# A hybrid attention and MLP block on one core: prefix and attention queues in another order, the weight splits of the attention on VectorE

## The chip, the cores and the metric

One NeuronCore of a Trainium2 chip runs the whole program. The metric is the device time of one execution in microseconds (us); for repeated runs the median is given. The engines are TensorE (PE), VectorE (DVE), ScalarE (ACT) and GpSimd (POOL), with SyncE (SP) for most DMA issues. Each works through its own queue in order, and they wait for each other by semaphores.

## What is computed

Two layers over one sequence of S = 512 tokens of width 1024, in fp32. Each layer computes (`x` the stream, cut from the reference):

```
xn = rms_norm(x, attn_norm)
nsa_q, kv_c, kv_s, kv_w, nsa_g, cq, ckv, k_rope_raw, gate_a, gate_b = split_cols(xn @ w_in)
o_a = nsa_attention(...)    # 8 heads, 2 KV groups: compressed, selected and window branch
o_b = mla_attention(...)    # 8 heads; q = rms_norm(cq) @ w_uq, kv = rms_norm(ckv) @ w_ukv, rope
merged = sigmoid(gate_a) * (o_a @ nsa_w_o) + sigmoid(gate_b) * (o_b @ mla_w_o)
x = x + merged @ w_out
x = x + square(relu(rms_norm(x, mlp_norm) @ w_up)) @ w_down
```

and a last `rms_norm` ends it. In the MLA branch every head's key has 64 columns of its own and 32 roped ones that all heads share (`k_pe`).

## The kernel before

**Splits.** PE multiplies in a rounded fp32 form (fp32r), and a product is made of three matmuls: high part by high part, high by rest, rest by high (L1447, L1448, L1449). So every operand is split once. A weight unit is 128x1024 fp32 (512 KB). SP loads it into one of two `stage` slots; ACT rounds it into `wsplit[:, 0]` (`split_hi`, L602); the rest, `stage` minus the rounded part, goes into `wsplit[:, 1]`. The rest is made by DVE (`split_lo`, L958) or by POOL (its `split_lo`, L495). Narrow units, for the compression weights, have slots of their own (`narrow`). All names ending in `_hi` are ACT's rounding copies, and those in `_lo` or `_rest` the subtractions on DVE or POOL.

**Prefix.** 29 items of the list `PREFIX` are projected one after another from the normed input: keys and values of the three branches (KC, VC, KS, V 0, KW, V 1), queries (Q 0 to 3), the MLA's inputs (CQ 0 to 2), MISC, five gates; the compression's units W1, W2K, W2V come between. At each item ACT and DVE run what the list's code puts there: evacuation, the next split, rotation of queries and keys (`swap`, L652, on ACT; `rotated`, L1031, L1035, L1043, on DVE), their splits (`q_hi`/`q_lo`, `k_hi`, `v_hi`/`v_lo`). POOL makes the key rests (L481). For the MLA's norm ACT squares the three CQ tiles into `csq` (L708); PE sums columns by matmuls against a vector of ones (`c_mean_squares`, L1589, fp32 matmuls of one column); ACT takes the root, DVE the reciprocal and diagonals (L1087, L1091), and PE spreads them (`c_spread`, L1597). `kc_hi` (ACT, L742) and `kc_lo` (DVE, L1132) split the compressed keys.

**Attention.** The loop has 106 steps for 96 jobs: 64 of the NSA branch, then 32 of MLA. A job passes through the steps by lags: scores S on PE and the row maximum on DVE (L1188) at its own step, exponentials on ACT (L771), the sum's reciprocal (DVE, L1193) and POOL's `scale` (L490) two steps later, both for two jobs at a time on even steps, the transposes T on PE (L1708) at 4, their split (ACT L766, DVE `probs_lo` L1198) at 5, the product with the values (L1732) at 7 and the output at 8. PE fills the gaps with the remaining projections: `FILL` gives four pieces of a unit to steps: gates first, `("MLA", 0)` behind GATE 11, more gates, then MLA 1, 2, WA 0, MLA 3, WA 1 to 3. An MLA unit projects queries (MQ), for `p < 2` also keys (MK) and values (MV) of head pairs; their evacuations run at the steps of `EMPTY_AT`: `mla_rotate` (DVE L1215), `mla_k` (L1237), `mla_v`.

`SPLIT_STEP` gives each of 20 units the step in which its slot is free: 0, 2, 6, 11, 16, 21, 27, 32, 37, 43, 48, 53, 65, 73, 79, 81, 87, 90, 96, 100. In the kernel before, POOL makes these rests at the top of the next step:

```
for u in SPLIT_STEP:
    if SPLIT_STEP[u] == i - 1:
        split_lo(u)
```

Behind it in a step POOL runs `scale` of two jobs, `output_rest` (L507), `mla_key_rest` (L516), loads and stores of gates, and `mla_query_rest` (L522). In `mla_begin(p)`, p < 2, ACT copies `k_pe` into the shared rows of `MK` (L792, twice) at the first step of MLA p, and POOL's `mla_key_rest(p)` makes their rests one step later. DVE's order in a step is: maximum, sums, `probs_lo`, small splits of the first steps (`vc_lo`, L1140, at 3), evacuations, `output_lo`, and in steps 3 to 8 `compressed_weights` (L1162 to L1177), which picks the selected blocks. PE's scores of job i wait for the maximum of job i - 2 and, for MLA jobs, for the query rest `MLO["MQ", ...]`.

**Behind the attention.** `mla_half`, the out tiles and the MLP in four quarters run with every split on DVE and little else there; POOL squares (L588).

Of the kernel before, what the change touches and what calls it, by code (L numbers as in the profile page):

```python
# [9 lines left out]
ALU = mybir.AluOpType  # L10
# [25 lines left out]
FIRST_GATE, EARLY = 5, 12  # L36
# [74 lines left out]

def tile_of(item, piece):

    name, i = item
    if name == "MLA":
        return [("MQ", i, 0), ("MQ", i, 1), ("MK", i, 0), ("MV", i, 0)][piece]
    if name == "WA":
        return ("A", 2 * i + piece // 2)
    return item
# [46 lines left out]
for i in range(STEPS):  # L166
    for t in EMPTY_AT[i] + EMPTY_AT[i - 1]:
        if (t[0] in ("MK", "MV")) == (t in EMPTY_AT[i]) and t[0] in ("MQ", "MK", "MV"):
            MHI[t] = len(MHI)
    for name, p in DURING + LATE:  # L170
        if name == "MLA" and p < 2:
            if FIRST_STEP[name, p] == i:
                MHI["PE", p] = len(MHI)
            if FIRST_STEP[name, p] == i - 1:
                MLO["PE", p] = len(MLO)
    for t in EMPTY_AT[i - 2]:
        if t[0] == "MQ":
            MLO[t] = len(MLO)
# [23 lines left out]
def build(nc, units, units_n, params, x_in, tables, cf32, cmasks, gates_dram, out):  # L202
    ctx = ExitStack()
    with ctx:
# [185 lines left out]
        s_csq, s_cms, s_crms, s_cdiag, s_cspread = sems("s_csq", "s_cms", "s_crms", "s_cdiag", "s_cspread")  # L390
        s_cf, s_chi, s_clo = sems("s_cf", "s_chi", "s_clo")
# [75 lines left out]
        def _(pool):  # L467
# [7 lines left out]
            for l in range(L):  # L475
# [34 lines left out]

                def mla_key_rest(p, scaled):
                    pool.wait_ge(s_scl, l * NJ + scaled)
                    u = max(v for v in SPLIT_STEP if SPLIT_STEP[v] <= FIRST_STEP["MLA", p])
                    split_done(pool, l, u)
                    pool.wait_ge(s_mhi, l * NMHI + (MHI["PE", p] + 1))
                    pool.tensor_tensor(MK[64:128, p % 2, :, 1, :], kpe[64:128, :].unsqueeze(1).broadcast_to([64, 2, S]),  # L516
                                       MK[64:128, p % 2, :, 0, :], ALU.subtract).then_inc(s_mlo, 1)
                    pool.wait_ge(s_mlo, l * NMLO + (MLO["PE", p] + 1))
# [29 lines left out]
                pool.wait_ge(s_kl, l * 2 + 2)  # L548
                for i in range(FIRST_GATE):
                    store_gate(i)  # L550

                for i in range(STEPS):
                    for u in SPLIT_STEP:
                        if SPLIT_STEP[u] == i - 1:
                            split_lo(u)
# [4 lines left out]
                    if 0 <= j < NJ - 1 and closes(j) is not None:  # L560
                        done = [u for u in SPLIT_STEP if SPLIT_STEP[u] < i]
                        if done:
                            split_done(pool, l, max(done))
                        output_rest(closes(j), min((i - LAG_SUM) // 2 * 2 + 2, NJ))
                    for p in range(2):
                        if FIRST_STEP["MLA", p] == i - 1:
                            mla_key_rest(p, (i - LAG_SUM) // 2 * 2 + 2)
# [31 lines left out]
        def _(act):  # L599
# [42 lines left out]
            for l in range(L):  # L642
# [145 lines left out]
                def mla_begin(p):  # L788
                    act.wait_ge(s_scores, l * NJ + QK_AFTER[p])
                    if p < 2:  # L790
                        for e in range(2):
                            ins = act.activation(MK[64:128, p, e, 0, :], kpe[64:128, :], ACT.Copy)  # L792
                        ins.then_inc(s_mhi, 1)
# [28 lines left out]
                for u, item in enumerate(PREFIX):  # L822
# [4 lines left out]
                    if 0 < u and u in BN and item != ("GATE", FIRST_GATE - 1) and (l, u) != (0, 1):  # L827
                        if name == "KW":
                            k_hi(0)
                        split_hi(l, BIG[BN[u] + 2])  # L830
# [5 lines left out]
                    if name == "KW":  # L836
                        copies(1)
                        swap(2)
                    if item == ("V", 1):
                        blocks_hi(1)  # L840
                        v_hi()
                        k_hi(1)
# [21 lines left out]
                    if item == ("GATE", 2):  # L864
                        kc_hi()
# [9 lines left out]
                for i in range(STEPS):  # L875
# [31 lines left out]
                    for p in range(PAIRS):  # L907
                        if FIRST_STEP["MLA", p] == i:
                            mla_begin(p)
                    if 10 <= i < 13:  # L910
                        c_hi(i - 10)
# [41 lines left out]
        def _(dve):  # L953
# [58 lines left out]
            for l in range(L):  # L1012
# [254 lines left out]
                for u, item in enumerate(PREFIX):  # L1267
# [40 lines left out]
                    if item == ("V", 1):  # L1308
                        blocks_lo(1)
                        v_lo()  # L1310
# [15 lines left out]
                    if item in ROPED and name != "KS":  # L1326
                        rotated(ROPED.index(item))
# [12 lines left out]
                for i in range(STEPS):  # L1340
                    if i < NJ:
                        max_of(i)
                    if i % 2 == 0 and 0 <= i - LAG_SUM < NJ:
                        sums_of(i - LAG_SUM)
                    if 0 <= i - LAG_SPLIT < NJ:
# [5 lines left out]
                    for t in EMPTY_AT[i]:  # L1351
# [6 lines left out]
                        if name == "MQ":  # L1358
                            mla_rotate(t[1], t[2])
# [7 lines left out]
                    if 0 <= j < NJ and closes(j) is not None:  # L1367
                        output_lo(closes(j))
                    if 3 <= i < 9:
# [75 lines left out]
        def _(pe):  # L1445
# [29 lines left out]
            for l in range(L):  # L1475
# [107 lines left out]
                def c_mean_squares():  # L1583
                    free(("CM", 0))
                    pe.wait_ge(s_csq, l * 3 + 3)
                    for kind, tiles in enumerate(((0, 1), (2,))):
# [105 lines left out]
                def scores(i):  # L1692
# [3 lines left out]
                    if i >= NSA_NJ and qt == QT - 1:  # L1696
                        pe.wait_ge(s_mlo, l * NMLO + (MLO["MQ", t, e] + 1))
# [300 lines left out]
```

## Time and profile before

| | before |
|---|---|
| median of 3 runs | 1541.52 us (1540.92 to 1542.46) |
| the profiled execution | 1544.23 us, of which the span is 1542.4 |
| PE busy in the span | 1510.6 us, 98% |
| DVE, ACT, POOL busy | 882.6, 717.9, 437.5 us |
| mean granted clock of TensorE | 0.996 of full speed |

The span goes from the first to the last instruction in the trace. Layer 0 has its prefix up to some 145 us, its attention to 365 and the rest to 775; layer 1 the same stages from there. "Idle before" is the time an engine stood before an instruction, and the arrow names what ended last among what it waited for. PE's matmuls overlap: one takes 0.39 us and the next begins 0.23 us after it.

### The profile page before, as it was taken

The page shows a single profiled execution, that of the slowest core. Times are in us where ns is not written, and L with a number is a line of the kernel's source. Part 1 is how long each engine was busy: PE and PEld are TensorE (multiplying, and loading weights), DVE is VectorE, ACT ScalarE, POOL GpSimd, SP SyncE. Part 2 cuts the span into 40 slices and gives each one's busy share as a digit, 9 for nine tenths or more (in the row PEclk, how much of TensorE's full clock was granted, in tenths as well). Part 3 has the DMA queues.
Part 4 walks back from the last instruction along what each step waited for, and adds up shares of the span by engine and source line. Part 5 has one row for each costly group of instructions (what it writes and reads, how often), then busy time and mean ns, then how long its engine had stood idle before and what let it go on. Part 6 is the DMA issues. An engine that isn't in the chain of part 4 may idle for free.

```text
span 1542.4 us, 21237 instructions
## 1 busy us (share of the span) xinstructions
PE 1510.6 (98%) x7412; PEld 1264.5 (82%) x7412; DVE 882.6 (57%) x1529; ACT 717.9 (47%) x1308; POOL 437.5 (28%) x455
## 2 busy tenths in 40 slices
PE   8999999999999999999999999999999999999998
PEld 6888888887888888888888788788878888888886
DVE  6864755766654444535557757566675535354453
ACT  6853777873432222222366547777644212222222
POOL 1301666775020100101021036768730201010011
PEclk9999999999999999999999999999999999999999
DMA  5333212125333323323323422122343333323233
GB/s 208 105 128 123 90 62 76 45 91 173 96 96 96 96 95 95 98 94 97 107 83 123 151 81 83 55 69 58 98 148 94 96 96 96 97 94 105 92 101 110
DMA packets 43363, 154.31 MB, mean 100 GB/s; under 512 B 5440, under 2 KB 5440, under 8 KB 43280
## 3 DMA queue, kind: packets, MB, share of 16 engines
q1 hardware_dynamic: 37296, 133.77, 27.9%
q0 software_dynamic: 5696, 18.94, 3.5%
q8 instruction: 48, 0.79, 0.2%
q10 hardware_dynamic: 288, 0.52, 0.1%
q14 instruction: 35, 0.29, 0.1%
HBM read 142.73 MB, written 10.49 MB: 99 GB/s over the span
## 4 chain that ended last, share of the span: by engine, by line
PE 85%; DVE 5%; ACT 4%; issue 4%; DMA 1%; POOL 1%; SPq 0%; POOLq 0%; DVEq 0%; ACTq 0%
PE G L1447 14%; PE G L1449 13%; PE G L1448 13%; PE O L1449 9%; PE O L1448 9%; PE O L1447 9%; PE O L1732 3%; PE T L1708 3%; PE S L1683 2%; PE T L1447 2%; PE T L1449 2%; PE T L1448 2%; PE O L1522 1%; ACT wsplit L602 1%; DVE F L1388 1%
## 5 line engine op out<-in xcount | busy, mean ns | idle before, releaser
L602 ACT ACTIVATE wsplit<-stage 128x1024 fp32r<-128x1024 f32 x227 | 240.2, 1058 | 606.7 <-PE G L1449 281.2
L958 DVE TENSOR_TENSOR wsplit<-stage,wsplit 128x1024 fp32r<-128x1024 f32 x178 | 256.8, 1443 | 72.9 <-ACT wsplit L602 72.7
L588 POOL TENSOR_TENSOR F<-Y 128x512 f32<-128x512 f32 x64 | 68.4, 1069 | 637.4 <-DVE Y L1405 637.4
L1447 PE MATMUL G<-xg,wsplit 128*128 128x512 f32 x592 | 237.9, 402 | 10.0 <-DVE wsplit L984 6.8
L1448 PE MATMUL G<-xg,wsplit 128*128 128x512 f32 x592 | 232.1, 392 | 0.0
L1449 PE MATMUL G<-xg,wsplit 128*128 128x512 f32 x592 | 231.9, 392 | 0.0
L495 POOL TENSOR_TENSOR wsplit<-stage,wsplit 128x1024 fp32r<-128x1024 f32 x48 | 115.8, 2412 | 128.1 <-ACT wsplit L602 126.9
L1188 DVE CUSTOM_DVE_ANT_0 F<-S,F 128x512 f32<-128x512 f32 x192 | 93.6, 488 | 98.7 <-PE S L1683 62.0
L1447 PEld LDWEIGHTS G<-xg,wsplit 128*128 128x128 f32 x592 | 112.0, 189 | 32.8 <-DVE wsplit L984 6.8
L771 ACT ACTIVATE F<-F,nmx 128x512 f32<-128x512 f32 x192 | 107.7, 561 | 64.3 <-DVE nmx L1188 62.9
L1449 PEld LDWEIGHTS G<-xg,wsplit 128*128 128x128 f32 x592 | 111.7, 189 | 24.5
L1448 PEld LDWEIGHTS G<-xg,wsplit 128*128 128x128 f32 x592 | 112.0, 189 | 20.9 <-issue 0.7
L1447 PE MATMUL G<-area,wsplit 128*128 128x512 f32 x320 | 124.7, 390 | 0.3
L1449 PE MATMUL G<-area,wsplit 128*128 128x512 f32 x320 | 124.5, 389 | 0.0
L1447 PE MATMUL O<-area,wsplit 128*128 128x512 f32 x320 | 124.5, 389 | 0.0
L1448 PE MATMUL O<-area,wsplit 128*128 128x512 f32 x320 | 124.5, 389 | 0.0
L1448 PE MATMUL G<-area,wsplit 128*128 128x512 f32 x320 | 124.5, 389 | 0.0
L1449 PE MATMUL O<-area,wsplit 128*128 128x512 f32 x320 | 124.5, 389 | 0.0
L1198 DVE TENSOR_TENSOR area_b<-T,area_b 128x512 fp32r<-128x512 f32 x192 | 92.8, 484 | 26.2 <-ACT area_b L766 23.9
L1447 PE MATMUL O<-xg,wsplit 128*128 128x512 f32 x256 | 99.6, 389 | 0.0
L1448 PE MATMUL O<-xg,wsplit 128*128 128x512 f32 x256 | 99.6, 389 | 0.0
L1449 PE MATMUL O<-xg,wsplit 128*128 128x512 f32 x256 | 99.6, 389 | 0.0
(291 smaller groups left out, 3005.3 us busy)
## 6 DMA issues: line engine op xcount, KB each, us to landing
stage<-units SPq DMA_DIRECT2D x229, 512.0 KB, 3.5
stage_n<-units_n SPq DMA_DIRECT2D x20, 512.0 KB, 3.6
gates<-Y POOLq DMA_DIRECT2D x32, 256.0 KB, 2.6
E<-gates POOLq DMA_DIRECT2D x24, 256.0 KB, 3.7
F<-gates POOLq DMA_DIRECT2D x8, 256.0 KB, 4.0
x<-x_in SPq DMA_DIRECT2D x3, 512.0 KB, 6.4
rope<-tables POOLq DMA_DIRECT2D x1, 768.0 KB, 6.9
out<-F SPq DMA_DIRECT2D x3, 256.0 KB, 2.3
```

The lines of the kernel that those rows point to most:

```text
L495: pool.tensor_tensor(wslot(u)[:, 1, :], staged(u), wslot(u)[:, 0, :], ALU.subtract)\
L588: pool.tensor_tensor(F[:, m % 2, :], Y[:, m % 2, :], Y[:, m % 2, :], ALU.mult)\
L602: act.activation(wslot(u)[:, 0, :], staged(u), ACT.Copy).then_inc(s_whin if u in SN else s_whi, 1)
L771: act.activation(prob(i, w), prob(i, w), ACT.Exp, bias=nmx[:, i % 4:i % 4 + 1], scale=-1.0, accum_out=sums[:, i % 4:i % 4 + 1]).then_inc(s ...
L958: dve.tensor_tensor(wslot(u)[:, 1, :], staged(u), wslot(u)[:, 0, :], ALU.subtract)\
L1188: dve.tensor_tensor_reduce(prob(i, w), score_tile(i), maskrow[:, S - w:S], -1.0, 1e38, ALU.add, ALU.min, nmx[:, i % 4:i % 4 + 1]).then_inc ...
L1198: dve.tensor_tensor(pt_view(slot, 1, qt), tp_view(j % 2, qt), pt_view(slot, 0, qt), ALU.subtract)\
L1447: pe.matmul(dst, a(0), b(0), start=first, stop=False)
L1448: pe.matmul(dst, a(0), b(1), start=False, stop=False)
L1449: return pe.matmul(dst, a(1), b(0), start=False, stop=last)
L1708: ins = pe.transpose(TP[j % 2][:, kt * P:(kt + 1) * P], prob(j, S)[:, kt * P:(kt + 1) * P], ident)
L1732: ins = pe.matmul(dst[:, kt * P:S], v, PT[:, slot, c, kt * S:(kt + 1) * S - kt * P], start=opens and c == 0, stop=closes(j) is not None an ...
```

## The change

1. **Splits of the attention.** POOL's loop no longer makes the 20 rests. DVE makes each at the end of the same step, after `output_lo` and before `compressed_weights`. POOL keeps its split for V 0 in the prefix and three behind the attention. Its waits on splits go; a wait `rests_done` for its own older query rests takes their place.
2. **MLA 0.** `EARLY` goes from 12 to 13: GATE 12 is projected in steps 32 to 36, and MLA 0 in 37 to 41 (before: MLA 0 in 32 to 36, GATE 12 behind it). Its evacuations move with it.
3. **Shared key rows.** ACT's two copies leave `mla_begin` and run at `KEY_STEP` = 43 and 69, and POOL's rests at 44 and 70; before, they ran at 32 and 65, and at 33 and 66. The scores of the MLA jobs now wait for the rest of their key pair by name too.
4. **DVE's order in a step.** `mla_rotate` comes ahead of `probs_lo`.
5. **Prefix.** ACT's `swap(2)` and DVE's `rotated(2)`, KW's rotation, move from KW's item to V 1's; `k_hi(1)` moves from V 1's item to Q 0's; `kc_hi` moves ahead of the split in GATE 2's item.
6. **The mean square of CQ.** POOL adds `csq[1]` to `csq[0]` once (128x512), behind its last key rest of the prefix, and PE sums the columns of two tiles instead of three: 8 fp32 matmuls instead of 12.

The tables and their steps:

```diff
-FIRST_GATE, EARLY = 5, 12
+FIRST_GATE, EARLY = 5, 13
...
+KEY_STEP = [FIRST_STEP["MLA", 0] + 6, FIRST_STEP["MLA", 1] + 4]
```

On POOL:

```diff
+                def rests_done(i):
+                    rests = [MLO[t] for t in MLO if t[0] == "MQ" and EMPTY[t] + 2 < i]
+                    if rests:
+                        pool.wait_ge(s_mlo, l * NMLO + (max(rests) + 1))
...
+                pool.wait_ge(s_csq, l * 3 + 2)
+                pool.tensor_tensor(csq[:, 0, :], csq[:, 0, :], csq[:, 1, :], ALU.add).then_inc(s_csum, 1)
                 for i in range(FIRST_GATE):
                     store_gate(i)
 
                 for i in range(STEPS):
-                    for u in SPLIT_STEP:
-                        if SPLIT_STEP[u] == i - 1:
-                            split_lo(u)
...
                     for p in range(2):
-                        if FIRST_STEP["MLA", p] == i - 1:
+                        if KEY_STEP[p] == i - 1:
+                            rests_done(i)
                             mla_key_rest(p, (i - LAG_SUM) // 2 * 2 + 2)
```

On ACT:

```diff
                     if 0 < u and u in BN and item != ("GATE", FIRST_GATE - 1) and (l, u) != (0, 1):
                         if name == "KW":
                             k_hi(0)
+                        if item == ("GATE", 2):
+                            kc_hi()
                         split_hi(l, BIG[BN[u] + 2])
...
                     if name == "KW":
                         copies(1)
+                    if item == ("V", 1):
                         swap(2)
-                    if item == ("V", 1):
                         blocks_hi(1)
                         v_hi()
+                    if item == ("Q", 0):
                         k_hi(1)
...
+                        if p < 2 and KEY_STEP[p] == i:
+                            mla_key_hi(p)
```

On DVE:

```diff
                     if item == ("V", 1):
+                        rotated(2)
                         blocks_lo(1)
                         v_lo()
...
+                    for t in EMPTY_AT[i]:
+                        if t[0] == "MQ":
+                            mla_rotate(t[1], t[2])
                     if 0 <= i - LAG_SPLIT < NJ:
                         probs_lo(i - LAG_SPLIT)
...
                         output_lo(closes(j))
+                    for u in SPLIT_STEP:
+                        if SPLIT_STEP[u] == i - 1:
+                            split_lo(l, u)
                     if 3 <= i < 9:
                         compressed_weights((i - 3) // 3, (i - 3) % 3)
```

On PE:

```diff
+                    pe.wait_ge(s_csum, l + 1)
-                    for kind, tiles in enumerate(((0, 1), (2,))):
+                    for kind, tiles in enumerate(((0,), (2,))):
...
                     if i >= NSA_NJ and qt == QT - 1:
-                        pe.wait_ge(s_mlo, l * NMLO + (MLO["MQ", t, e] + 1))
+                        pe.wait_ge(s_mlo, l * NMLO + (max(MLO["MQ", t, e], MLO["PE", min(t, 1)]) + 1))
```

The lines of the changed kernel stand a little lower: DVE's L958 is its L966, L1140 its L1148, L1162 its L1170, L1188 its L1196, L1198 its L1206; POOL's L490 is its L493, L507 its L510, L516 its L522, and L522 its L528.

The order of DVE's instructions in layer 0's steps 3 and 4, before (`vblk` is `vc_lo`'s result, ISA with `nmx` the row maximum):

```order
L1140 TENSOR_TENSOR vblk<-O,vblk 32x2x64 x4
L1162 TENSOR_TENSOR E<-E,constf 128x512
L1188 ISA F,nmx<-S,F 128x512
L1188 ISA nmx 128x1
L1193 RECIPROCAL rsum<-sums 128x2
L1165 TENSOR_REDUCE small<-E 128x16
L1167 TENSOR_SCALAR small<-small 128x16
L1169 RECIPROCAL small<-small 128x16
L1188 ISA F,nmx<-S,F 128x384
L1188 ISA nmx 128x1
L1198 TENSOR_TENSOR area_b<-T,area_b 128x4x128
```

and now:

```order
L1148 TENSOR_TENSOR vblk<-O,vblk 32x2x64 x4
L966 TENSOR_TENSOR wsplit<-stage,wsplit 128x1024
L1170 TENSOR_TENSOR E<-E,constf 128x512
L1196 ISA F,nmx<-S,F 128x512
L1196 ISA nmx 128x1
L1201 RECIPROCAL rsum<-sums 128x2
L1173 TENSOR_REDUCE small<-E 128x16
L1175 TENSOR_SCALAR small<-small 128x16
L1177 RECIPROCAL small<-small 128x16
L1196 ISA F,nmx<-S,F 128x384
L1196 ISA nmx 128x1
L1206 TENSOR_TENSOR area_b<-T,area_b 128x4x128
```

One row is new there, the weight unit's rest between `vc_lo` and `compressed_weights`; the row maxima and `probs_lo` come one instruction later.

POOL's order around the second key rest, before (`F<-F,rsum` rows are `scale`, `area<-kpe,area` the key rest, `area<-E,area` the query rests, `wsplit` a weight unit's rest):

```order
L495 TENSOR_TENSOR wsplit<-stage,wsplit 128x1024
L490 TENSOR_SCALAR F<-F,rsum 128x512
L490 TENSOR_SCALAR F<-F,rsum 128x384
L516 TENSOR_TENSOR area<-kpe,area 64x2x512
L490 TENSOR_SCALAR F<-F,rsum 128x256
L490 TENSOR_SCALAR F<-F,rsum 128x128
L522 TENSOR_TENSOR area<-E,area 128x512 x2
L490 TENSOR_SCALAR F<-F,rsum 128x512
L490 TENSOR_SCALAR F<-F,rsum 128x384
L490 TENSOR_SCALAR F<-F,rsum 128x256
```

and now, from the same `scale` rows before the query rests on:

```order
L493 TENSOR_SCALAR F<-F,rsum 128x256
L493 TENSOR_SCALAR F<-F,rsum 128x128
L528 TENSOR_TENSOR area<-E,area 128x512 x2
L493 TENSOR_SCALAR F<-F,rsum 128x512
L493 TENSOR_SCALAR F<-F,rsum 128x384
L522 TENSOR_TENSOR area<-kpe,area 64x2x512
L493 TENSOR_SCALAR F<-F,rsum 128x256
L493 TENSOR_SCALAR F<-F,rsum 128x128
L510 TENSOR_TENSOR xg<-F 64x512
L493 TENSOR_SCALAR F<-F,rsum 128x512
```

The weight unit's rest is gone, and the key rest has moved from before the query rests to the middle of the scales four steps later.

## Rows read from the trace of the kernel before

**Rows 1.** The page, part 1: busy us, share of the span, instructions.
```profile
PE 1510.6 (98%) x7412; PEld 1264.5 (82%) x7412; DVE 882.6 (57%) x1529; ACT 717.9 (47%) x1308; POOL 437.5 (28%) x455
```

**Rows 2.** Busy time by stretch: start:end, length, each engine's busy (instructions), PEclk, DMA, GB/s.
```profile
145.00:365.00 220.00, 213.51 (x1204) 182.31 (x1203) 141.15 (x422) 159.91 (x390) 153.64 (x168) 1.00 0.24 79
```

**Rows 3.** What PE waited for: line <- releaser: total us, times, longest.
```profile
PE G L1447 <- DVE wsplit L984: 6.8, 1, 6.8
PE T L1708 <- DVE area_b L1198: 5.0, 10, 1.3
PE G L1447 <- DVE E L1215: 2.9, 4, 1.1
PE G L1447 <- DVE wsplit L958: 2.6, 2, 1.5
```

**Rows 4.** Timeline at `kc_lo`: start, us, engine, line [idle before <-releaser].
```profile
122.42 1.06 ACT L602 ACTIVATE wsplit<-stage 128x1024 fp32r<-128x1024 f32 x1 [3.39 <-PE G L1449]
124.21 0.59 PE L1564 MATMUL G<-area_b,area 128*128 128x32 f32 x4 [0.94 <-DVE area_b L1132]
```

**Rows 5.** Timeline of PE, the one-column matmuls of each layer.
```profile
81.45 3.14 PE L1589 MATMUL T<-ones,csq 128*128 128x1 f32 x24
...
842.19 2.73 PE L1589 MATMUL T<-ones,csq 128*128 128x1 f32 x24
```

**Rows 6.** Windows of PE: start:end, length, PE busy, PEclk, DMA, GB/s.
```profile
83.60:90.40 6.80, 6.80 (x24) 0.50 0.00 0
...
844.80:848.20 3.40, 3.40 (x14) 0.50 0.02 8
```

**Rows 7.** Timeline, the diagonals and the matmul that needs them.
```profile
90.38 1.29 DVE L1091 TENSOR_TENSOR csq<-constf,crc 128x512 f32<-128x512 f32 x2 [0.15 <-DVE crc L1087]
93.74 0.59 PE L1597 MATMUL G<-csq,ones 128*128 128x512 f32 x1
```

**Rows 8.** Timeline, the narrow split and its PE matmuls.
```profile
73.34 1.22 DVE L958 TENSOR_TENSOR narrow<-stage_n,narrow 128x1024 fp32r<-128x1024 f32 x1
75.03 0.40 PE L1522 MATMUL O<-narrow,area_b 128*128 128x256 f32 x2
```

**Rows 9.** Timeline, PE and DVE between CQ 0 and CQ 1.
```profile
52.09 0.50 PE L1447 MATMUL G<-xg,wsplit 128*128 128x512 f32 x1 [1.50 <-DVE wsplit L958]
61.73 1.21 DVE L958 TENSOR_TENSOR wsplit<-stage,wsplit 128x1024 fp32r<-128x1024 f32 x1
63.15 0.40 PE L1447 MATMUL T<-xg,wsplit 128*128 128x512 f32 x1
```

**Rows 10.** A split beside POOL (timeline); groups by line, 145 to 365 us.
```profile
440.46 1.84 DVE L958 TENSOR_TENSOR wsplit<-stage,wsplit 128x1024 fp32r<-128x1024 f32 x1 [0.46 <-ACT wsplit L602]
L495 POOL TENSOR_TENSOR wsplit<-stage,wsplit 128x1024 fp32r<-128x1024 f32 x21 | 50.3, 2395 | 25.3 <-ACT wsplit L602 25.2
L1188 DVE CUSTOM_DVE_ANT_0 F<-S,F 128x512 f32<-128x512 f32 (+1 forms) x96 | 46.8, 488 | 49.4 <-PE S L1683 31.2 <-PE S L1689 17.5 <-DVE F L1149 0.3
```

**Rows 11.** Timeline around MLA 0, POOL and PE.
```profile
220.52 2.40 POOL L516 TENSOR_TENSOR area<-kpe,area 64x1024 fp32r<-64x1024 f32 x1
223.98 0.66 PE L1708 MATMUL T<-constf,F 128*128 128x128 f32 x4 [0.87 <-POOL F L490]
232.05 0.30 PE L1708 MATMUL T<-constf,F 128*128 128x128 f32 x1 [1.29 <-DVE area_b L1198]
```

**Rows 12.** Timeline around MLA 1, POOL and PE.
```profile
287.97 2.53 POOL L522 TENSOR_TENSOR area<-E,area 128x512 fp32r<-128x512 f32 x2
290.48 1.25 POOL L490 TENSOR_SCALAR F<-F,rsum 128x512 f32<-128x512 f32 x2
291.55 0.48 PE L1687 MATMUL S<-area 128*128 128x512 f32 x1
```

**Rows 13.** DVE in steps 3 to 7: a window's busy time, and a timeline row.
```profile
157.00:165.30 8.30, 7.73 (x23) 1.00 0.30 96
165.31 1.66 DVE L1167 TENSOR_SCALAR small<-small 128x16 f32<-128x16 f32 x1
```

More of the change, by code:

```diff
@@ L169 @@
             MHI[t] = len(MHI)
[L170 to L175, printed above, removed]
+    for p in range(2):
+        if KEY_STEP[p] == i:
+            MHI["PE", p] = len(MHI)
+        if KEY_STEP[p] == i - 1:
+            MLO["PE", p] = len(MLO)
     for t in EMPTY_AT[i - 2]:
@@ L390, in build @@
         s_csq, s_cms, s_crms, s_cdiag, s_cspread = sems("s_csq", "s_cms", "s_crms", "s_cdiag", "s_cspread")
+        s_csum = sem("s_csum")
         s_cf, s_chi, s_clo = sems("s_cf", "s_chi", "s_clo")
@@ L509, in output_rest @@
                     pool.wait_ge(s_olo, l * NHEAD + (n + 1))
+                def rests_done(i):
+                    rests = [MLO[t] for t in MLO if t[0] == "MQ" and EMPTY[t] + 2 < i]
+                    if rests:
+                        pool.wait_ge(s_mlo, l * NMLO + (max(rests) + 1))
                 def mla_key_rest(p, scaled):
                     pool.wait_ge(s_scl, l * NJ + scaled)
-                    u = max(v for v in SPLIT_STEP if SPLIT_STEP[v] <= FIRST_STEP["MLA", p])
-                    split_done(pool, l, u)
                     pool.wait_ge(s_mhi, l * NMHI + (MHI["PE", p] + 1))
@@ L560, in _ @@
                     if 0 <= j < NJ - 1 and closes(j) is not None:
-                        done = [u for u in SPLIT_STEP if SPLIT_STEP[u] < i]
-                        if done:
-                            split_done(pool, l, max(done))
+                        rests_done(i)
                         output_rest(closes(j), min((i - LAG_SUM) // 2 * 2 + 2, NJ))
                     for p in range(2):
-                        if FIRST_STEP["MLA", p] == i - 1:
+                        if KEY_STEP[p] == i - 1:
+                            rests_done(i)
                             mla_key_rest(p, (i - LAG_SUM) // 2 * 2 + 2)
@@ L789, in mla_begin, with mla_key_hi @@
                     act.wait_ge(s_scores, l * NJ + QK_AFTER[p])
[L790 to L793, printed above, removed]
+                def mla_key_hi(p):
+                    for e in range(2):
+                        ins = act.activation(MK[64:128, p, e, 0, :], kpe[64:128, :], ACT.Copy)
+                    ins.then_inc(s_mhi, 1)
                 def mla_q(p, e):
@@ L863, in _ @@
                         q_hi(3)
-                    if item == ("GATE", 2):
-                        kc_hi()
                     if item == ("W1", 7):
@@ L1325, in _ @@
                         hidden(0)
-                    if item in ROPED and name != "KS":
+                    if item in ROPED and name not in ("KS", "KW"):
                         rotated(ROPED.index(item))
@@ L1357, in _ @@
                             evac(t, t, Y[:, t[1] % 2, :])
-                        if name == "MQ":
-                            mla_rotate(t[1], t[2])
                         if name == "MK":
```

## The prediction

> **What bounds the kernel now.** I read the busy shares first. TensorE (PE) computes for 1510.6 us of a span of 1542.4 us, VectorE (DVE) for 882.6, ScalarE (ACT) for 717.9, GpSimd (POOL) for 437.5 [rows 1]. No PE matmul is removed apart from 32 tiny ones, so the change can only win from the 31.8 us in which PE idles and from places where it runs slowly. Next the stretches. Between 145 and 365 us, the first layer's attention, PE idles 6.5 us, DVE is busy 141.2 of 220 us, ACT 159.9, POOL 153.6; the second layer's attention is alike [rows 2]. The change leaves the MLP's code alone. So what pays is in the prefix and the attention, and each occurs twice. Third, what PE waited for [rows 3]: 6.8 us for the kernel's very first split, which the change doesn't touch; 5.0 in ten waits for `probs_lo` (L1198); 2.9 in four for `mla_rotate` (L1215); 2.6 in two for a prefix split (L958). Some 15 us are in reach of a reordering, not all of it aimed at. Below, "per layer" is doubled in the sum.
>
> **kc_hi moved ahead of GATE 2's split.** ACT's split at 122.42 waits 3.39 us for PE to leave a slot, and `kc_hi`, whose input is older, stands behind it; DVE's `kc_lo` comes after both, and PE starts at 124.21 after 0.94 us idle [rows 4]. Ahead of the split it is over some 4 us earlier. The gap and the slow first matmul go: 0.94 + 0.16 = 1.1 per layer, **-2.2**. Nothing queues behind it that the 0.21 us would hurt.
>
> **One sum in place of four matmul pairs.** 12 fp32 matmuls of one column stand in the trace as 24 rows and take 3.14 us in layer 0 and 2.73 in layer 1 [rows 5]. A wait for the new POOL sum can't bind, since it is ready some 8 us before. A third of the rows goes: 1.05 + 0.91, **-2.0**.
>
> **The clock behind them.** Right after these matmuls, with no PE idle, the granted clock is 0.50 (1.2 GHz) for 6.8 us in layer 0 and 3.4 us in layer 1, against 1.00 (2.4 GHz) before [rows 6]. At half speed half of these stretches is lost, 3.4 + 1.7 us. Sixteen such rows instead of 24 may or may not keep it up; I think they do, more likely than not: layer 1's shorter burst already lost half as long. The gain is capped: PE's `c_spread` at 93.74 needs DVE's diagonals, which end at 91.67 [rows 7], 2.1 us before; that chain runs on DVE and ACT and doesn't speed up with PE's clock. I take 1.8 + 1.0, **-2.8**. Ends: 0 if the clock falls all the same, -5.1 if nothing caps it. The Trainium skill ("TensorE: Matmul & The Clock Gate", Part 1) puts the clock down to how busy PE has lately been; by that a shorter stretch of such matmuls can only help, and whether this one is short enough no row shows.
>
> **The price of the sum.** POOL gets a 128x512 add of two SBUF tensors, 1.27 us by a pair of that size (L522, 2.53 for two) [rows 12]. It can start near 72 us, when DVE has `q_lo` before it and then the narrow split, which ends 0.5 us before PE wants it at 75.03 [rows 8]. Beside a POOL instruction a split is stretched, 1.84 us [rows 10] against 1.22 [rows 8]. Bounds 0 and 1.3 per layer; I take 0.6, nearest to the stretch of a split: **+1.2**.
>
> **KW's rotation one item later, k_hi(1) two.** This frees DVE before CQ 0's split; PE's 1.50 us wait at 52.09 [rows 9] and its like of 1.09 in layer 1 [rows 3] go. But DVE is busy from then to the CQ 1 split at 61.73, which ends 0.2 us before PE's first matmul for it, the next item's start at 63.15 [rows 9]. PE 1.5 us earlier finds that split late, and the moved work sits in the same stretch. The wait moves, it isn't gone: ends -2.6 and +2; taken **+0.2**.
>
> **The rests moved from POOL to DVE.** 21 POOL splits cost 50.3 us of POOL's 153.6 in the attention at 2.40 us each [rows 10]; 20 per layer go. DVE pays 1.22 alone, 1.84 where POOL runs a scale beside it: 24 to 37 us per layer. DVE has 78.9 us idle there [rows 2], so most is absorbed: before its 96 row maxima (L1188) it idles 49.4 us, 0.5 each [rows 10], and a step lasts 2.1 us, so a split is caught up within three or four steps, while PE asks for a step's results about two steps later. In steps 3 to 10, however, DVE doesn't rest: it is busy 7.73 of 8.30 us from 157 us on [rows 13]. Three splits land there (ends of steps 1, 3 and 7). The second stands behind `vc_lo` and delays everything after; the third is partly paid for by L1167, 1.66 us beside POOL's split, 0.18 without [rows 13]. I take one whole split plus a third, 1.6 per layer (0.8 to 2.5): **+3.2**. The Trainium skill ("GPSIMD Engine Reference", section 8, Key points) says that GpSimd shares its SBUF interfaces with VectorE and that DVE instructions with two SBUF inputs contend. The stretched rows agree, and that rule speaks against the move: a split has two such inputs and now meets the scales. It would fit the upper ends; its own outcome is rival C.
>
> **MLA 0 five steps later, mla_rotate first.** Around MLA 0 POOL runs a split, an output rest and the key rest at 220.52 (2.40 us) back to back, its scale is late and PE waits 0.87 at 223.98; later it waits 1.29 for `probs_lo` at 232.05 [rows 11]. With two shorter waits between and the slow first matmuls behind each, I count 3.3 per layer. POOL's part goes (no split, key rest elsewhere). The burst of MK, MV and MQ evacuations on DVE stays, five steps on, with a split at each end. I take -2.5: **-5.0** (ends -6.6 and 0). For MLA 2, the wait on `mla_rotate` behind `probs_lo` goes (0.6 per layer, within the 2.9 of [rows 3]): **-1.2**. MLA 3's stays: POOL's split there ended no later than DVE's would.
>
> **The second key rest.** The copies go to step 69, POOL's rest to step 70 behind scale(68) and scale(69). In the trace these end at 291.7 and the rest takes 2.40 [rows 11], so it ends near 294.1; PE wants to start the scores at 291.55 [rows 12], and now waits for that rest by name. POOL has shed the old rest's 2.4 us and a split's 2.4 by then, but the scales wait for DVE's sums, not only for POOL. On the other side two waits at MLA 1, of L1215's and L1198's [rows 3], shrink. Ends per layer -1 (POOL fully early) and +2.5; I take +1.75: **+3.5**.
>
> **Sum.** -2.2 - 2.0 - 2.8 + 1.2 + 0.2 - 5.0 - 1.2 + 3.2 + 3.5 = -5.1 us. The profiled execution took 1544.2, 2.7 above the median of 1541.5, so the change is put on the median: 1536.4, given as 1536.5. Late next: `probs_lo` in steps 3 to 10 and the key rest at step 70.
>
> **Rivals.** What a measurement here can tell from no change is 0.2%, 3.1 us.
> A. Helpers keep up: the key rest is in time (0 instead of +3.5) and the early splits cost 1.0 in all instead of 3.2. For it: 50 us off POOL. Against it: the DVE busy 93% of the time there [rows 13]. -5.1 - 3.5 - 2.2 = -10.8: 1530.7. Chance 0.22.
> B. The clock falls all the same, with 16 rows as with 24: +2.8, 1539.3, no change that can be told. For it: layer 1 falls with a shorter burst. Chance 0.2.
> C. The other side: DVE becomes the bound of the attention. Three early splits at the stretched 1.84 fully on the path (11.0 instead of 3.2), and the two splits about MLA 0 at 1.22 take back its 5.0. -5.1 + 7.8 + 4.9 = +7.6: 1549.1. It decides once a split is longer than what DVE idles in the next two steps, 1.0 us on the mean, and PE's order leaves nothing more. DVE's 36% idle speaks against it. Chance 0.14.
> D. The change doesn't do what it says for PE: the MLA 0 waits only move five steps on with their burst, +5.0: 1541.4. Chance 0.1.
> The forecast itself has 0.34; in its own range of 1533 to 1540 some falls above 1538.4. Faster by over 0.2% is A, most of the forecast and a third of B: 0.61. Within it: the rest of these and D, 0.24. Slower 0.15. Range: 1529.5, a little beyond A for its missed sizes, to 1543, which holds D and leaves out C.
>
> **What would show it.** No wait at `kc_lo`; 16 rows after 81 us taking 2.0 us; PEclk 1.00 behind them; a PE wait of 1 to 2.5 us for POOL's key rest in step 72's scores; `probs_lo` waits growing in steps 4 to 10; none of POOL's scale near MLA 0. Wrong would be: waits for DVE splits in the middle of the attention, or POOL named nowhere.

## The result and the profile after

| | before | after |
|---|---|---|
| median of 6 runs | 1541.52 us (1540.92 to 1542.53) | 1546.96 us (1545.88 to 1548.24) |
| ratio | | 1.003, 95% interval 1.0019 to 1.0041 |
| the profiled execution | 1544.23, span 1542.4 | 1546.04, span 1544.2 |

The change made the kernel slower by 5.4 us. The forecast was 1536.5, and the range ended at 1543. The two profiled executions differ by 1.8 us only: the one of before was 2.7 above its median, that of after 0.9 below. Both matter below.

The page of the changed kernel, part 1, answers to [rows 1]:

```profile
PE 1510.4 (98%) x7396; PEld 1262.7 (82%) x7396; DVE 932.9 (60%) x1569; ACT 716.7 (46%) x1308; POOL 360.4 (23%) x417
```

PE works as long as before. DVE has 50 us more and POOL 77 less. The windows of the first attention answer to [rows 2] (columns as there):

```profile
145.00:365.00 220.00, 212.05 (x1188) 180.67 (x1187) 163.10 (x439) 156.91 (x386) 112.85 (x147) 0.99 0.25 79
```

DVE went from 141 to 163 us of 220, POOL from 154 to 113. No engine is full. What PE waited for answers to [rows 3]:

```profile
PE T L1722 <- DVE area_b L1206: 7.5, 12, 1.4
PE G L1460 <- DVE wsplit L992: 6.9, 1, 6.9
PE S L1701 <- POOL area L522: 3.2, 2, 1.6
PE T L1460 <- DVE wsplit L966: 2.3, 2, 1.2
PE G L1460 <- DVE area L1245: 1.7, 2, 0.9
PE O L1535 <- DVE narrow L966: 0.9, 2, 0.5
```

The waits for `mla_rotate` (2.9 us) and `kc_lo` (1.9) are gone, and so is POOL's scale. In their place the waits for `probs_lo`, now L1206, went from 5.0 to 7.5 us, and 3.2 us for POOL's key rest (L522), 2.3 for prefix splits in another place, 1.7 for MLA's key evacuation (L1245) and 0.9 for the narrow split are new.

Where the time went is best seen from one row, DVE's row maximum, which both kernels have once per job. It is two instructions, the search and the read-out into `nmx`; the table has the start of the read-out in layer 0, in us:

| job | before | after | difference |
|---|---|---|---|
| 0 | 146.89 | 143.24 | -3.65 |
| 6 | 162.28 | 159.71 | -2.57 |
| 36 | 222.46 | 219.52 | -2.94 |
| 48 | 249.57 | 245.95 | -3.62 |
| 66 | 280.74 | 277.19 | -3.55 |
| 72 | 293.30 | 291.89 | -1.41 |
| 90 | 335.46 | 335.55 | +0.09 |

The rows of job 72, before and after (timeline of DVE):

```profile
293.30 0.08 DVE L1188 DVE_READ_ACCUMULATOR2_ANT nmx<- 128x1 f32 x1
```

```profile
291.89 0.08 DVE L1196 DVE_READ_ACCUMULATOR2_ANT nmx<- 128x1 f32 x1
```

The prefix gained 3.65 us in this pair of executions. The early steps gave back 1.1, MLA 0 gained 0.7, and between jobs 66 and 90 all was lost: 3.6 us. Layer 1 shows the same with a smaller gain ahead of it: -2.13 us at job 66, +1.75 at job 90.

The late loss begins here, in PE's, POOL's and ACT's timeline at job 72:

```profile
289.47 0.77 PE L1701 MATMUL S<-area 128*128 128x512 f32 x1 [1.61 <-POOL area L522]
```

```profile
287.02 2.35 POOL L522 TENSOR_TENSOR area<-kpe,area 64x1024 fp32r<-64x1024 f32 x1
```

```profile
285.16 1.15 ACT L797 ACTIVATE area<-kpe 64x512 fp32r<-64x512 f32 x2
```

ACT copies the shared key rows behind step 69's exponentials, POOL's key rest follows from 287.02 to 289.37, and PE, idle from 287.86, stands 1.61 us. Right behind that the granted clock falls, in both layers (windows of PE: start:end, length, PE busy, PEclk, DMA, GB/s):

```profile
285.70:289.10 3.40, 2.00 (x17) 1.00 0.00 0
289.10:292.50 3.40, 3.03 (x11) 0.50 0.00 0
292.50:296.00 3.50, 3.50 (x21) 1.00 0.01 2
1046.80:1050.20 3.40, 1.64 (x14) 1.00 0.00 0
1050.20:1053.70 3.50, 3.50 (x12) 0.51 0.00 0
```

In the 3.4 us before each fall PE was busy for 2.00 and 1.64 us. Then comes 0.50 (1.2 GHz) for 3.4 us, which costs 1.7 by my estimate, half of the stretch. In the kernel before, neither place shows a fall. The Trainium skill ("TensorE: Matmul & The Clock Gate", Part 1) says that the gate follows how busy PE has lately been, and these rows agree: the wait of 1.6 us costs itself and then a stretch at half speed. The falls of [rows 6] are another case, for no idle of PE stands ahead of them.

### The profile page after: what moved, and what is told of

Its sections match the earlier page's. It is cut to its first block, busy times and chain, and to the rows that moved or that the text cites. A ratio compares the mean times of both kernels' runs of the same rounds, so it can differ in the third digit from the quotient of the medians.

```text
span 1544.2 us, 21201 instructions
## 1 busy us (share of the span) xinstructions
PE 1510.4 (98%) x7396; PEld 1262.7 (82%) x7396; DVE 932.9 (60%) x1569; ACT 716.7 (46%) x1308; POOL 360.4 (23%) x417
## 4 chain that ended last, share of the span: by engine, by line
PE 80%; DVE 8%; ACT 5%; issue 4%; POOL 1%; DMA 1%; POOLq 0%; DVEq 0%; SPq 0%; ACTq 0%
PE G L1460 13%; PE G L1461 13%; PE G L1462 13%; PE O L1461 9%; PE O L1462 9%; PE O L1460 8%; PE T L1722 3%; PE O L1746 3%; PE S L1697 2%; ACT F L656 1%; DVE wsplit L966 1%; PE T L1460 1%; PE T L1462 1%; PE T L1461 1%; PE O L1535 1%
## 5 line engine op out<-in xcount | busy, mean ns | idle before, releaser
L966 DVE TENSOR_TENSOR wsplit<-stage,wsplit 128x1024 fp32r<-128x1024 f32 x218 | 318.3, 1460 | 73.5 <-ACT wsplit L606 73.2
L1196 DVE CUSTOM_DVE_ANT_0 F<-S,F 128x512 f32<-128x512 f32 x192 | 93.2, 485 | 70.2 <-PE S L1697 43.6
L493 POOL TENSOR_SCALAR F<-F,rsum,gt 128x512 f32<-128x512 f32 (+3 forms) x128 | 89.7, 707 | 130.7 <-DVE rsum L1201 130.7
L1206 DVE TENSOR_TENSOR area_b<-T,area_b 128x512 fp32r<-128x512 f32 x192 | 92.5, 482 | 25.1 <-ACT area_b L770 23.0
```

The costliest lines, as they stand in the source:

```text
L493: pool.tensor_scalar(p, p, rsum[:, j % 8:j % 8 + 1], gt[:, qt, col:col + 1] if j < NSA_NJ else 1.0, ALU.mult, ALU.mult).then_inc(s_scl, 1)
L966: dve.tensor_tensor(wslot(u)[:, 1, :], staged(u), wslot(u)[:, 0, :], ALU.subtract)\
L1196: dve.tensor_tensor_reduce(prob(i, w), score_tile(i), maskrow[:, S - w:S], -1.0, 1e38, ALU.add, ALU.min, nmx[:, i % 4:i % 4 + 1]).then_inc ...
L1206: dve.tensor_tensor(pt_view(slot, 1, qt), tp_view(j % 2, qt), pt_view(slot, 0, qt), ALU.subtract)\
```

## The experiments

All times are medians of 4 to 11 executions. They were taken in four groups, each beside the kernel before, whose median was 1542.2 for a_key66, a_pool, a_early12 and a_rotlast; 1542.15 for a_pool_key66, b_splits, b_prefix and a_nosum; 1543.06 for a_k66_early, a_k66_mla, best_sumlate and b_order; 1542.92 for a_key45_66; and 1541.52 beside the changed kernel itself. So a difference between runs of separate groups is good to about 1 us. I give the bare difference of the medians, and where it matters also the difference of the distances, each run's from the kernel before of its own group.

### The key rest three steps earlier

```diff
-KEY_STEP = [FIRST_STEP["MLA", 0] + 6, FIRST_STEP["MLA", 1] + 4]
+KEY_STEP = [43, 66]
```

> The changed kernel with the second key copies at step 66 instead of 69, so POOL's second key rest at step 67. Theory K (the new wait of the scores on POOL's key rest, 1.6 us per layer in the changed kernel's trace, and the 3.4 us at clock 0.50 that follow it, which cost 1.7): both go in both layers, about 1540.4 against 1547.0, that is a ratio to the kernel before of 0.999. Rival D (VectorE with the splits is the bound there): the wait for the key rest goes but one for probs_lo takes its place, 1545 to 1547, ratio 1.003.

Measured: 1539.18 us (1538.75 to 1540.16), ratio 0.9977 (0.9968 to 0.9986). Theory K holds. One number changed makes the slower kernel faster than the one before. In the changed kernel POOL idles 3.12 us between the scales of jobs 65 and 66, where the rest now runs (timeline of POOL, a_key66):

```profile
280.61 2.73 POOL L522 TENSOR_TENSOR area<-kpe,area 64x1024 fp32r<-64x1024 f32 x1 [0.59 <-ACT area L797]
```

No wait for it is left and no clock fall in the attention. The 7.8 us gained (8.5 by the distances) are more than the 6.6 expected. The mean granted clock of the timed executions went from 0.995 to 0.999, so I take it that some of them had longer falls than the profiled one; their traces aren't there.

### The splits back on POOL

```diff
+                    for u in SPLIT_STEP:
+                        if SPLIT_STEP[u] == i - 1:
+                            split_lo(u)
                     if i % 2 == 0 and 0 <= i - LAG_SUM < NJ:
                         scale(i - LAG_SUM)
```

and the same three lines taken from DVE's loop, with POOL's waits on its own splits before it reads the same rows.

> The changed kernel with the 20 splits per layer given back to POOL at the top of their steps, all else as changed. Rival D: the 0.7 us per layer lost in the early steps and some 1.3 per layer lost at MLA 2 and 3 come back, about 1543, ratio 1.001. Theory K: POOL is later still at the key rest (a split of 2.4 us at step 66 lies ahead), the wait for it stays at 1.6 us or grows to 3, 1545 to 1549, ratio 1.003 to 1.005.

Measured: 1538.59 us (1537.51 to 1540.49), ratio 0.9973 (0.9964 to 0.9983). Both halves came: the wait for the key rest grew to 1.9 us per layer, and still the kernel is 8.4 us faster than the changed one (9.1 by the distances), more than rival D had said. What PE waited for, and its windows at clock 0.50, in this run:

```profile
PE S L1704 <- POOL area L525: 3.8, 2, 1.9
PE T L1725 <- DVE area_b L1212: 2.5, 8, 0.7
```

```profile
285.40:292.20 6.80, 5.89 (x18) 0.50 0.00 0
1043.20:1046.50 3.30, 2.77 (x10) 0.50 0.00 0
```

The waits for `probs_lo` are 2.5 us instead of 7.5. So two costs stand beside each other, and the next run takes both away.

> The changed kernel with the 20 splits per layer back on POOL and the second key copies at step 66. Theory S+K (two separate costs of the change: the splits on VectorE, 8.4 us, and the late key rest with its slow clock, 7.8 us): the run with the splits on POOL still waits 1.9 us per layer for the key rest and has 6.8 and 3.4 us at clock 0.50 behind it, so 1538.6 - 3.8 - 5.1 = 1529.7, ratio 0.992. Rival O (the two overlap: with splits on POOL its split at step 66 makes the key rest at 67 late too): 1535 to 1538, ratio 0.996 to 0.998.

Measured: 1529.98 us (1529.11 to 1531.84), ratio 0.9919 (0.9900 to 0.9937). The two costs add: 8.4 and 7.8 make 16.2, and this run is 17.0 below the changed kernel. It is 12.2 us faster than the kernel before, with PE's waits at

```profile
PE T L1463 <- DVE wsplit L972: 3.1, 3, 1.2
PE T L1725 <- POOL F L493: 1.5, 2, 0.7
...
PE T L1725 <- DVE area_b L1212: 0.8, 4, 0.2
```

### The splits on VectorE, alone

> The kernel before with part 1 of the change alone: its 20 splits per layer on VectorE at the end of their step, everything else as before (MLA 0 at step 32, keys at 32 and 65, old order in the prefix and of mla_rotate). Theory S: the splits cost by themselves, in the early steps 0.7 to 1.1 us per layer and about the MLA units 2.6 and more: 1549 to 1553, ratio 1.005 to 1.007. Rival: they cost only together with the moved MLA 0, since POOL's late scale at 223.98 goes with them: 1540 to 1543, ratio 1.000.

Measured: 1555.79 us (1554.58 to 1558.25), ratio 1.0089 (1.0066 to 1.0111). Slower still than theory S said: 13.6 us, from part 1 alone. What PE waited for there:

```profile
PE T L1716 <- DVE area_b L1203: 12.6, 14, 1.5
...
PE G L1455 <- DVE E L1220: 4.6, 8, 1.1
PE G L1455 <- DVE area L1242: 2.8, 2, 1.4
```

12.6 us for `probs_lo` against 5.0 before, 4.6 against 2.9 for `mla_rotate`, 2.8 against 0.6 for the key evacuation: 11.5 us more, less 1.7 for POOL's scale, which PE no longer waits for. The rest of the 13.6 I can't place. PE waits for no split in the attention: the loss that the rows show is booked under the work that stands behind one.

### Where the splits cost

The next two give only some splits back to POOL, by their steps:

```diff
+                        if SPLIT_STEP[u] == i - 1 and i - 1 in (0, 2, 6, 11):
+                            split_lo(u)
```

> a_key66 (changed kernel, second key copies at step 66) with only the four early splits per layer, those of steps 0, 2, 6 and 11, back on POOL. Of the 9.2 us per execution between a_key66 (1539.2) and a_pool_key66 (1530.0) the prediction's theory put nearly all of the splits' cost in the early steps: then 1531. The traces say 1.1 us per layer there (PE's wait of 0.94 and 0.12 for the split behind vc_lo): 1537.0, ratio 0.9965.

Measured: 1538.08 us (1537.52 to 1539.07), ratio 0.9964 (0.9950 to 0.9977): 1.1 us gained of 9.2, or 2.0 by the distances. So the early steps aren't where the splits cost most.

> a_key66 with only the eight splits per layer next to MLA units (those of steps 32, 37, 43, 65, 73, 79, 81 and 87) back on POOL, twelve left on VectorE. If the splits cost where VectorE also has the MLA's evacuations and rotations, 2.2 us per layer about MLA 0 and 1.6 about MLA 1 to 3 by the traces: 1531.6, ratio 0.993. If it is the sum of 20 small delays: 8 of 20 of 9.2 us, 1535.5, ratio 0.9955.

Measured: 1531.48 us (1530.86 to 1532.58), ratio 0.9921 (0.9905 to 0.9938): 7.7 of 9.2, or 8.6 by the distances, the first case. The eight splits beside the MLA units carry most of the cost, the twelve others 1.5 at most. The traces say the same by place: PE waits 7.4 us more in the attention of a_key66 than in that of a_pool_key66, both layers together, of which 2.7 for `probs_lo` at step 44, 1.9 for it in the early steps and 1.7 for the key evacuation (L1245).

One of the eight stands out in the trace of the changed kernel. POOL's first key rest, then DVE, then PE:

```profile
237.64 2.39 POOL L522 TENSOR_TENSOR area<-kpe,area 64x1024 fp32r<-64x1024 f32 x1
```

```profile
237.78 3.33 DVE L966 TENSOR_TENSOR wsplit<-stage,wsplit 128x1024 fp32r<-128x1024 f32 x1
241.03 0.55 DVE L1196 CUSTOM_DVE_ANT_0 F<-S,F 128x384 f32<-128x384 f32 x1
```

```profile
242.34 0.41 PE L1722 MATMUL T<-constf,F 128*128 128x128 f32 x2 [1.37 <-DVE area_b L1206]
```

A split takes 1.22 us alone. This one begins 0.14 us behind POOL's key rest and takes 3.33: its end is 1.08 us after the rest's, at 240.03. The row maximum and `probs_lo` behind it are late, and PE waits 1.37 us (1.40 in layer 1). The change had put both at step 44.

```diff
-KEY_STEP = [43, 66]
+KEY_STEP = [45, 66]
```

> a_key66 with the first key copies at step 45 instead of 43, so that POOL's first key rest (2.39 us, step 46) no longer runs beside VectorE's split of step 44. In the trace of the changed kernel that split takes 3.33 us and PE then waits 1.37 and 1.40 us for probs_lo. Theory P (the two engines exclude each other, and the split waits for the key rest to end): the split takes 1.22 us, the waits go, 1539.2 - 2.8 = 1536.4, and up to 1 us more for the slow matmuls behind. Rival B (the burst of MLA 0's evacuations makes DVE late there anyway): the split is short but the wait for probs_lo stays above 1 us, 1538.5 to 1539.5.

Measured: 1536.16 us (1535.65 to 1536.30), ratio 0.9954 (0.9941 to 0.9968): 3.0 us (3.7 by the distances), theory P. The split now, and what POOL runs beside it (timelines of DVE and POOL):

```profile
237.10 1.22 DVE L966 TENSOR_TENSOR wsplit<-stage,wsplit 128x1024 fp32r<-128x1024 f32 x1
```

```profile
237.14 2.03 POOL L493 TENSOR_SCALAR F<-F,rsum,gt 128x256 f32<-128x256 f32 x2 [0.29 <-DVE rsum L1201]
```

The load on DVE is the same, and both waits of PE at this place are gone. So a third of the splits' cost was this meeting. The Trainium skill ("SBUF — State Buffer", section "SBUF: two separate sides") describes it: a VectorE instruction with two SBUF inputs and a GpSimd instruction that reads SBUF take the shared ports as an exclusive lock, and whichever starts first keeps it to its end. The rows agree in both directions. The split has a neighbour here too, two `scale` rows, but it starts 0.04 us ahead of them, and they wait: 2.03 us for the two, against 0.98 in the changed kernel. Where a `scale` starts first the split waits, only for less long. In the changed kernel, for example:

```profile
277.55 1.25 POOL L493 TENSOR_SCALAR F<-F,rsum 128x512 f32<-128x512 f32 x2 [0.93 <-DVE rsum L1201]
```

```profile
278.32 1.55 DVE L966 TENSOR_TENSOR wsplit<-stage,wsplit 128x1024 fp32r<-128x1024 f32 x1
```

This split ends 1.07 us behind the second scale's end at 278.80. The 19 splits of that attention other than the one at step 44 take between 1.21 and 1.68 us: POOL's long instruction is what made one meeting dear, not the number of its inputs.

### The other parts

> The changed kernel with EARLY back at 12 (MLA 0 in steps 32 to 36, GATE 12 behind it), the keys still at 43 and 69. If the position of MLA 0 matters, its waits (0.87 and 1.37 us per layer in the changed kernel's trace) go or grow: I expect them to be about the same size five steps earlier, within 1 us of 1547.0, ratio 1.003. If the move was what saved the 0.6 to 0.8 us per layer that the trace shows there, 1548.4, ratio 1.0045.

Measured: 1551.75 us (1550.91 to 1553.53), ratio 1.0057 (1.0043 to 1.0071). Worse than either case: 4.8 us more than the changed kernel (4.1 by the distances), so moving MLA 0 was a real gain. What PE waited for `probs_lo` there, against 7.5:

```profile
PE T L1722 <- DVE area_b L1206: 11.4, 16, 1.4
```

In layer 0 PE waits 0.64, 0.80 and 1.31 us at MLA 0 and 1.40 at step 44 there, against 0.87 and 1.37 with MLA 0 moved. MLA 0's burst and the collision at step 44 are two separate places there; I take it that with MLA 0 moved they are partly one.

> The changed kernel with mla_rotate behind probs_lo again. If that order was a gain, PE's waits for mla_rotate come back at MLA 1 and 2 (1.1 and 0.4 us per layer): 1549 to 1550, ratio 1.005. If it delays probs_lo (which PE waits for at 242.34 and 285.15 in the changed kernel, 1.4 and 0.9 us), the time falls: 1544 to 1545, ratio 1.002.

Measured: 1548.81 us (1548.23 to 1550.66), ratio 1.0039 (1.0026 to 1.0053). The order with `mla_rotate` first is worth 1.9 us by the medians and 1.2 by the distances, little more than such a comparison can tell. Its waits, in this run:

```profile
PE G L1459 <- DVE E L1223: 4.6, 6, 1.4
```

They came back, but not where I had expected them: 1.44 us at 230.67 and 1.45 at 992.59, beside MLA 0, and none at MLA 1.

> The kernel before with parts 5 and 6 alone (prefix order and the sum of csq on POOL), and the scores' wait for the key rest by name. By the prediction's prefix terms -2.2 - 2.0 + 1.2 + 0.2 = -2.8, and -2.8 more for the clock: 1542.0 - 5.6 = 1536.4, ratio 0.996. If the timed executions of the kernel before mostly lack the fall of the clock that its profiled one shows, only the first -2.8: 1539.2, ratio 0.998.

Measured: 1539.53 us (1539.00 to 1541.59), ratio 0.9981 (0.9971 to 0.9990). A gain of 2.6 us: the second of the two forecasts.

> The kernel before with part 5 alone (swap(2), rotated(2), k_hi(1) and kc_hi moved), no sum on POOL. By the prediction's terms -2.2 for kc_hi and +0.2 for the rest: 1540.1, ratio 0.9987. b_prefix, which had the sum too, was 1539.5, so the sum is worth 2.0 of PE less its 0.9 of waits and what of the clock it saves in some executions: 1540.1 to 1541. The profile should show clock 0.50 behind the 24 one-column rows in at least one layer.

Measured: 1542.62 us (1539.90 to 1546.31), ratio 0.9996 (0.9985 to 1.0007). The order alone can't be told from no change, though the wait for `kc_lo` is gone in its trace. Two things stand against the gain. The ten executions have a mean clock of 0.9964, the 16 of the kernel before beside them 0.9976. And two waits of 1.1 to 1.2 us for the CQ 1 split took the place of those at CQ 0, and a third of 1.1 for an early prefix split stood near 21 us in this execution; that one varies between executions of one order, 0 to 1.4 us in the profiles of this study. The clock fell in both layers (windows of PE):

```profile
77.00:84.00 7.00, 7.00 (x43) 1.00 0.73 269
84.00:91.00 7.00, 7.00 (x31) 0.76 0.00 0
838.00:845.00 7.00, 7.00 (x43) 0.82 0.43 153
845.00:852.00 7.00, 7.00 (x24) 0.69 0.28 89
```

and with POOL's sum, in b_prefix, in neither:

```profile
84.00:91.00 7.00, 7.00 (x45) 1.00 0.19 75
...
845.00:852.00 7.00, 6.30 (x27) 1.00 0.31 88
```

Over all profiles of this study the clock fell behind 24 one-column rows in seven of eight passes through a prefix (before, b_splits and b_order twice, a_nosum once), and behind 16 in none of 22. b_order and a_nosum have the new prefix order too, so it isn't the order that keeps the clock up.

> The changed kernel without part 6: PE does all 12 one-column fp32 matmuls, POOL no sum. If the sum is worth its 2.0 us of PE less 1.2 for the narrow split (PE waits 0.44 and 0.48 us for that in the changed kernel): 1547.8, ratio 1.0035. The profile should show clock 0.50 behind the one-column matmuls where the 24 rows bring it down, and 1.00 if it was the order of the prefix that kept it up; with the fall 1549.5, ratio 1.0045.

Measured: 1549.16 us (1547.50 to 1550.22), ratio 1.0041 (1.0027 to 1.0056). The sum is worth 2.2 us in the changed kernel and 3.1 between b_order and b_prefix by the medians; by the distances it is 1.6 and 2.2. In a_nosum's profile the clock falls behind the 24 rows in layer 0 and not in layer 1.

> a_pool_key66 with POOL's sum of csq held until VectorE has done the narrow split of the second W1 unit. If the sum's price is the stretch of q_lo (2.40 us beside it, 1.39 without) that makes PE wait 0.46 us for the narrow split in each layer: 1530.0 - 0.9 = 1529.1. If the split is late anyway by the new order of the prefix: 1530.0. The difference is near what five rounds can tell; the trace decides by the wait at the first narrow matmuls.

```diff
+                split_done(pool, l, SMALL[1])
                 pool.wait_ge(s_csq, l * 3 + 2)
                 pool.tensor_tensor(csq[:, 0, :], csq[:, 0, :], csq[:, 1, :], ALU.add).then_inc(s_csum, 1)
```

Measured: 1530.28 us (1528.22 to 1530.80), ratio 0.9911 (0.9896 to 0.9925). PE's wait for the narrow split is gone from the trace, so its cause was the stretch beside the sum; the time can't be told from the 1529.98 without it.

## Why the prediction was wrong

The runs form a chain from the kernel before to the changed one, beside which the prediction's terms can be put:

| part | predicted | measured | by |
|---|---|---|---|
| prefix, sum and clock | -5.6 | -2.6 | b_prefix less before |
| MLA 0, `mla_rotate` (measured with the early key step) | -6.2 | -9.6 | a_pool_key66 less b_prefix |
| the splits on VectorE | +3.2 | +9.2 | a_key66 less a_pool_key66 |
| the key rest at step 70 | +3.5 | +7.8 | after less a_key66 |

The measured column adds up to +4.8, against 5.4. That the two are near follows from the chain itself; the 0.6 are what the kernel before differs by between groups. The independent tests are a_pool and b_splits.

- **Bound and places.** Right: nothing outside prefix and attention moved. From layer 1's last row maximum to the end of the span both kernels take some 438 us.
- **kc_hi (-2.2), one sum (-2.0), its price (+1.2), KW's rotation (+0.2).** Each happened in the trace as said: no wait at `kc_lo`, the one-column matmuls a third shorter (1.84 us in both layers), 0.44 and 0.48 us of waiting for the narrow split, and the wait of CQ 0 back at CQ 1, 1.08 us in layer 0 and 1.23 in layer 1:

```profile
57.63 0.50 PE L1460 MATMUL T<-xg,wsplit 128*128 128x512 f32 x1 [1.08 <-DVE wsplit L966]
```

  New, and not in the sum: PE waits 0.7 us per layer for the diagonals before `c_spread` (I had this as a cap on the clock's gain).
- **The clock behind the sum (-2.8).** The mechanism holds, and rival B with it falls: 16 rows, no fall. In the changed kernel's windows, which answer to [rows 6], the clock stays up:

```profile
84.00:91.00 7.00, 6.80 (x35) 1.00 0.07 5
...
845.00:852.00 7.00, 6.56 (x33) 1.00 0.07 6
```

  But the term was read from one execution and put on the median of others. The profiled execution of before, with 10.2 us at 0.50 and a mean clock of 0.996, was 2.7 above that median: most timed executions had lost less to the clock. In 61 runs of the kernel before beside the experiments the times spread from 1540.8 to 1547.7 us and the mean clocks from 0.995 to 1.000, with a mean of 0.998. The step that failed is "so the change is put on the median". On the median the prefix gained 2.6, not 5.6.
- **The rests on VectorE (+3.2).** The main error: 9.2 beside the other parts, 13.6 alone. One row was misread, too: the 1.84 us of [rows 10] is a split beside POOL's square (L588, from 440.18 to 441.22), not beside a scale. The early price was about right. The second split behind `vc_lo` did delay everything, as the rows of DVE and PE say:

```profile
152.15 1.19 DVE L1148 TENSOR_TENSOR vblk<-O,vblk 32x128 fp32r<-32x128 f32 x4 [1.56 <-ACT vblk L753]
153.37 1.22 DVE L966 TENSOR_TENSOR wsplit<-stage,wsplit 128x1024 fp32r<-128x1024 f32 x1
```

```profile
158.79 0.30 PE L1722 MATMUL T<-constf,F 128*128 128x128 f32 x1 [0.94 <-DVE area_b L1206]
```

  0.94 us and 0.12 ahead of it per layer; given back to POOL, the early splits gave 1.1 to 2.0 in all. What failed is "most is absorbed". The 0.5 us of idle before each row maximum is a mean over 96, and it says nothing of the steps where an MLA unit's evacuations, rotations and key pieces are in the queue: given back to POOL, the eight splits beside these gave 7.7 of the 9.2. How much idle each of the eight found isn't measured. DVE's busy share alone doesn't tell: it is 9.02 of 11.00 us from 231 to 242 in the changed kernel, a smaller share than the 93% of the early steps in [rows 13], where the splits cost some 2 us at most. I had priced the MLA parts with "a split at each end" of the burst and gave the splits no term there.
- **MLA 0 and mla_rotate (-5.0 and -1.2).** Without the splits these parts gave -9.6 with the early key step. In the changed kernel they are hidden, much as rival D has it: MLA 0 gained 0.7 us in layer 0, because the key evacuation (1.7 us for both layers) and the meeting of split and key rest took its place.
- **The key rest at step 70 (+3.5).** The place and the wait were right: 1.6 us per layer against 1.75. Left out was what the wait does to the clock, 1.7 us more per layer in the profile. Removing both gave 7.8.
- **The rivals.** The outcome is rival C's side, with part of its mechanism: DVE as what ends last. Its price sat in the wrong place, in the early steps. The Trainium skill's rule on the shared interfaces ("GPSIMD Engine Reference", section 8, Key points), which I cited as speaking against the move, was worth a term: 3.0 us came from a single pair of instructions in each layer.
- **The signs.** Those for the forecast came: PE's wait for the key rest in step 72's scores, `probs_lo` waits in the early steps, none of POOL's scale near MLA 0. Those for being wrong did not, though it was wrong: no wait names a DVE split in the attention. A split that makes others late isn't waited for itself.

## What to carry to other kernels

Work moved from a helper with idle time to one that has more of it on the mean still costs where the second has a burst: place it against the queue of each step, and look which long instructions it will run beside on the engine that shares its memory ports. When a new wait makes PE stand for 1.6 us, as here, price the clock behind it too. And a clock fall in a profiled execution is a fact of that execution; before its removal is counted against a median, compare the two times.

## What the runs showed of the hardware

- A 128x1024 subtraction on VectorE with two SBUF inputs took 1.22 us alone, 3.33 when it started 0.14 us behind a 2.39 us GpSimd subtraction, and ended 1.08 us after it; with that neighbour away it took 1.22 again. Started 0.04 us ahead of a pair of GpSimd scales it took 1.22, and they took 2.03 instead of 0.98.
- PE's wait of 1.6 us behind other short ones was followed by 3.4 us at clock 0.50 in both layers; with 1.9 us of waiting (a_pool) by 6.8 and 3.4. All ten waits for the late key rest, of 1.47 to 1.91 us, were followed by a fall (after, a_pool, a_early12, a_rotlast, a_nosum). Of 29 other waits of 1.29 to 1.53 us in the attention, one was: in a_rotlast PE waited 1.44 us in layer 0 and 1.45 in layer 1 at the same place, and the clock fell in layer 1 alone.
- 24 fp32 matmul rows of one column, 2.7 to 3.1 us with no idle, were followed by 3.4 or 6.8 us at clock 0.50 in seven of eight passes; 16 rows, 1.84 us, in none of 22.
- Executions of one kernel on one chip differ by up to 6.9 us (the kernel before, 1540.80 to 1547.72), and the longest have the lowest mean clocks: b_order spread from 1539.9 at a mean clock of 0.999 to 1546.3 at 0.994.
